# A hybrid decoder block on one core: projections as one plain float32 product in pairs of 64 columns, in place of three fp32r passes

## The reference

```python
h = rms_norm(x, mix_norm_w[l])
proj = h @ w_in[l]                      # 1024 x 7744: z, xbc, dt, q, k/v pairs, gates
y_ssm = mamba2_mixer(z, xbc, dt_raw, ...)
y_nsa = nsa_mixer(q, k_c, v_c, k_s, v_s, k_w, v_w, nsa_gate, ...)
g_ssm, g_nsa = jnp.split(jax.nn.sigmoid(merge_gate), 2, axis=-1)
merged = g_ssm * (y_ssm @ w_branch_ssm[l]) + g_nsa * (y_nsa @ w_branch_nsa[l])
x = x + merged @ w_out[l]
h = rms_norm(x, ffn_norm_w[l])
x = x + moe_ffn(h, ...)                 # 32 experts: top 4 of each token, gate_up 1024x2048, down 1024x1024
```

## Time and profile before

| | us |
|---|---|
| median of 3 runs | 1250.74 |
| lowest, highest | 1250.71, 1251.38 |
| profiled execution, its own time | 1250.38 |
| its span, first to last instruction | 1248.7 |

### The profile page before, as it was taken

One profiled execution on the slowest core, in us unless ns is written; L12 is line 12 of the kernel. 1 busy time (PEld: TensorE's weight loads), 2 busy tenths in 40 slices (PEclk: granted clock), 3 DMA queues, 4 the chain that ended last, 5 costly groups with the idle time before them and its releaser, 6 DMA issues.

```text
span 1248.7 us, 16280 instructions
## 1 busy us (share of the span) xinstructions
PE 1189.7 (95%) x6644; PEld 623.0 (50%) x6644; DVE 437.2 (35%) x869; ACT 287.7 (23%) x521; POOL 110.4 (9%) x97
## 2 busy tenths in 40 slices
PE   8999999999999999999898989899999999999996
PEld 8999988788743434433342424333343434243432
DVE  7776667767331231312122221212221212122212
ACT  6574457653410101101010100010110101010112
POOL 2302213345400000000000000000000000000000
PEclk9999999999999999999999999999999999999999
DMA  8747434339999999999999999999999999999996
GB/s 272 209 145 233 161 110 135 102 103 393 398 421 400 435 415 433 432 429 430 434 430 434 430 434 429 431 434 431 434 428 434 431 431 432 430 436 428 424 428 248
DMA packets 61565, 453.58 MB, mean 363 GB/s; under 512 B 9160, under 2 KB 33872, under 8 KB 45392
## 3 DMA queue, kind: packets, MB, share of 16 engines
q1 hardware_dynamic: 61216, 452.75, 88.3%
q10 hardware_dynamic: 304, 0.20, 0.1%
HBM read 451.88 MB, written 1.05 MB: 363 GB/s over the span
## 4 chain that ended last, share of the span: by engine, by line
PE 63%; DMA 29%; DVE 3%; ACT 3%; issue 1%; POOL 0%; SPq 0%; DVEq 0%; ACTq 0%
PE psum L1311 23%; DMA ring<-in_w_gate_up_dram 14%; DMA slot<-in_w_gate_up_dram 12%; PE psum L1323 11%; PE psum L940 9%; PE psum L1281 5%; PE psum L906 4%; PE psum L1349 3%; PE psum L842 3%; DMA ring<-in_w_down_dram 3%; PE psum L943 2%; ACT WH L1482 1%; ACT XDT L1661 1%; PE psum L1191 1%; DVE XDT L2139 1%
## 5 line engine op out<-in xcount | busy, mean ns | idle before, releaser
L1311 PE MATMUL psum<-ring,ZS 128*64 128x512 f32 x1512 | 344.7, 600 | 13.9 <-DMA ring<-in_w_gate_up_dram 13.5
L1311 PEld LDWEIGHTS psum<-ring,ZS 128*64 128x64 f32 x1512 | 105.0, 137 | 217.2 <-issue 194.3
L2285 DVE TENSOR_TENSOR X<-X,psum 128x1024 f32<-128x1024 f32 x62 | 72.9, 1217 | 370.8 <-PE psum L1349 370.7
L1323 PE MATMUL psum<-ring,HT 128*64 128x512 f32 x736 | 173.3, 625 | 22.6 <-DMA ring<-in_w_down_dram 22.6
L2267 DVE TENSOR_SCALAR ZS<-psum 128x512 f32<-128x512 f32 x32 | 22.1, 691 | 300.9 <-PE psum L1311 300.9
L1311 PE MATMUL psum<-slot,ZS 128*64 128x512 f32 x512 | 116.5, 597 | 7.7 <-DMA slot<-in_w_gate_up_dram 7.7
L1323 PEld LDWEIGHTS psum<-ring,HT 128*64 128x64 f32 x736 | 59.1, 143 | 129.5 <-issue 128.6
L1799 DVE TENSOR_TENSOR WL<-ring,WH 128x2048 fp32r<-128x2048 f32 (+1 forms) x42 | 95.9, 2285 | 37.9 <-ACT WH L1482 37.6
L1711 ACT ACTIVATE HT<-psum 128x512 f32<-128x512 f32 x31 | 18.5, 597 | 318.2 <-PE psum L842 318.2
L1482 ACT ACTIVATE WH<-ring 128x2048 fp32r<-128x2048 f32 (+1 forms) x42 | 78.9, 1878 | 9.8 <-PE psum L906 6.8
L1311 PEld LDWEIGHTS psum<-slot,ZS 128*64 128x64 f32 x512 | 34.4, 137 | 74.2 <-issue 58.8
(11 more groups left out here) (380 smaller groups left out, 1215.8 us busy)
## 6 DMA issues: line engine op xcount, KB each, us to landing
ring<-in_w_gate_up_dram SPq DMA_DIRECT2D x38, 4096.0 KB, 29.4
ring<-in_w_down_dram SPq DMA_DIRECT2D x18, 4096.0 KB, 30.8
slot<-in_w_gate_up_dram SPq DMA_DIRECT2D x12, 4096.0 KB, 28.9
ring<-in_w_gate_up_dram SPq DMA_DIRECT2D x15, 2048.0 KB, 13.4
ring<-in_w_in_dram SPq DMA_DIRECT2D x29, 1024.0 KB, 7.2
slot<-in_w_down_dram SPq DMA_DIRECT2D x7, 4096.0 KB, 30.8
ring<-in_w_down_dram SPq DMA_DIRECT2D x9, 2048.0 KB, 14.7
slot<-in_w_gate_up_dram SPq DMA_DIRECT2D x8, 2048.0 KB, 13.8
```

Source lines behind the costliest of these rows:

```text
L1311: ins = mm(psum[64 * (c % 2):64 * (c % 2) + 64, c // 2, :], XTS[:, k, s], every_other_run(row, c), start=False, stop=(k == KT - 1))
L1323: ins = mm(psum[64 * h:64 * h + 64, 2, :], lhs, w[:, at:at + 512], start=(k == 0), stop=(k == 7))
L2285: v.tensor_tensor(xo, xo, psum[:, 3 + 2 * t:5 + 2 * t, :], ALU.add).then_inc(o_read, 1)
```

## The change

All three-pass projections become one plain float32 product, with the stationary operand cut in two halves of 64 columns that write partitions 0 to 63 and 64 to 127 of the same bank. The splits on ScalarE and VectorE go, with their buffers, tokens and semaphores. The other float32 matmuls with 128 stationary columns named above are cut the same way. SyncE waits for a unit to be done before it loads its slot again, and issues four expert loads of 2 MB among the projection loads, at `mg` 4, `mg` 6, `bs` 0 and `bs` 2; the other early expert loads go out later in the order.

```diff
                 if u >= STREAM:
-                    if u - STREAM in SPLIT_UNITS:
-                        low_ready(sp, SPLIT_UNITS.index(u - STREAM))
-                    else:
-                        sp.wait_ge(unit_done, u - STREAM + 1)
+                    sp.wait_ge(unit_done, u - STREAM + 1)
                 full = ring_full[u % STREAM]
+                if (kind, m) in ahead:
+                    ahead[(kind, m)]()
...
+            ahead = {("mg", 4): lambda: load_half(gate_up_rows(0, 1), 1, 0),
+                     ("mg", 6): lambda: load_half(gate_up_rows(0, 1), 1, 1),
+                     ("bs", 0): lambda: early_load(1, 0), ("bs", 2): lambda: early_load(1, 1)}
...
             sp.wait_ge(pool_set, 3)
             sp.dma_start(once_row, unit_rows(3, 0, 4)[:, 2048:2 * 2048]).then_inc(once_full, 16)
-            sp.wait_ge(unit_done, at_unit[("bn", 3)] + 1)
-            load_half(gate_up_rows(0, 1), 1, 0)
-            low_ready(sp, len(SPLIT_UNITS) - 3)
-            low_ready(sp, len(SPLIT_UNITS) - 2)
-            early_load(0, 1)
             sp.wait_ge(mt_full, 4)
             once_quarter(0)
-            sp.wait_ge(unit_done, at_unit[("wo", 1)] + 1)
-            early_load(1, 0)
-            low_ready(sp, len(SPLIT_UNITS) - 4)
-            low_ready(sp, len(SPLIT_UNITS) - 1)
+            sp.wait_ge(unit_done, at_unit[("wo", 2)] + 1)
+            early_load(0, 1)
+            sp.wait_ge(unit_done, NU)
             early_load(0, 0)
-            sp.wait_ge(unit_done, at_unit[("wo", 2)] + 1)
-            early_load(1, 1)
-            sp.wait_ge(unit_done, NU)
-            load_half(gate_up_rows(0, 1), 1, 1)
...
                 if t == 0:
-                    pe.wait_ge(wh_ready, i + 2)
-                for n, (w, src) in enumerate([(wh, high), (wh, low), (wl, high)]):
-                    if w is wl and t == 0:
-                        low_ready(pe, i)
-                    if n == 1 and kind == "wo":
-                        pe.wait_ge(mt_low, 2 * h + t + 1)
-                    for k in range(4):
-                        ins = mm(bank(b, 512), src[:, 4 * h + k, P * t:P * t + P], w[:, k, :],
-                                 start=(h == 0 and n == 0 and k == 0), stop=(h == 1 and n == 2 and k == 3))
+                    pe.wait_ge(ring_full[u % STREAM], full_at[u])
+                for k in range(4):
+                    for c in (0, 64):
+                        ins = mm(bank(b, 512)[c:c + 64], src[:, 4 * h + k, P * t + c:P * t + c + 64], w[:, k, :],
+                                 start=(h == 0 and k == 0), stop=(h == 1 and k == 3))
...
+                thirds = (0, 3, 6, KT)
+                for k in range(thirds[n0], thirds[n1]):
+                    for c in (0, 64):
+                        at = slice(P * half + c, P * half + c + 64)
                         if feature_major:
-                            ins = mm(bank(b, 2, SEQ)[:, half], w[:, k, rows], src[:, k, :],
-                                     start=(n == 0 and k == 0), stop=(n == 2 and k == KT - 1))
+                            ins = mm(bank(b, 2, SEQ)[c:c + 64, half], w[:, k, at], HTH[:, k, :],
+                                     start=(k == 0), stop=(k == KT - 1))
...
-                mm(bank(7, SEQ), HTH[:, 0, 0:P], HTH[:, 1, :], start=True, stop=True)
+                mm(bank(7, SEQ)[0:64], HTH[:, 0, 0:64], HTH[:, 1, :], start=True, stop=True)
...
-            def split(u):
-
-                i = SPLIT_UNITS.index(u)
-                act.wait_ge(ring_full[u % STREAM], full_at[u])
-                if i >= SPLITS:
-                    act.wait_ge(unit_done, SPLIT_UNITS[i - SPLITS] + 1)
-                n = KT * (64 if UNITS[u][0] == "small" else 256)
-                a(WH[i % SPLITS][:, 0:n], slot_view(u, n), ACT.Copy).then_inc(wh_ready, 1)
...
-            def split(u):
-
-                i = SPLIT_UNITS.index(u)
-                dve.wait_ge(wh_ready, i + 2)
-                n = KT * (64 if UNITS[u][0] == "small" else 256)
-                v.tensor_tensor(WL[i % SPLITS][:, 0:n], slot_view(u, n), WHF[i % SPLITS][:, 0:n], ALU.subtract
-                                ).then_inc(wl_ready, 1)
...
```

More of the change, by code:

```diff
@@ L78 @@
 NU = len(UNITS)
-SPLIT_UNITS = [u for u, (kind, _) in enumerate(UNITS) if kind not in ("w1k", "w1v")]
 def wide(u):
@@ L165, in token_order @@
     out += [("H0", last), ("XX", 2), ("H1", last), ("RM", 2), ("P0", last), ("X3", 0), ("P1", last)]
[L168 to L178, removed]
-        else:
[L180 to L187, removed]
+    return out
 TOKENS = token_order()
@@ L286, in hybrid_block @@
         slot_at = [ring_at + 4 * SLOT * i for i in range(RING)]
[L287 to L298, removed]
+        HTH = at_place("HTH", [P, KT, SEQ], ht_at, F32)
+        OTH = at_place("OTH", [P, KT, SEQ], zs_at, F32)
+        YSH = at_place("YSH", [P, KT, SEQ], ec_at, F32)
         places = [at_place("slot0", [P, BIG], xdt_at + 4 * D, F32)[:]]
@@ L857, in first_unit @@
             def first_unit():
-                b = bank_of[0]
-                wh, wl = part(WH[0], 0, KT, 256), part(WL[0], 0, KT, 256)
+                b, w = bank_of[0], slot_view(0, KT, 256)
                 for part_n in range(2):
[L862 to L878, removed]
+                    pe.wait_ge((first_in, ring_full[0])[part_n], 16)
+                    for k in range(4 * part_n, 4 * part_n + 4):
+                        pe.wait_ge(ht_act, k // 2 + 1)
+                        for half in range(2):
+                            for c in (0, 64):
+                                ins = mm(bank(b, 2, SEQ)[c:c + 64, half], w[:, k, P * half + c:P * half + c + 64],
+                                         HTH[:, k, :], start=(k == 0 and half == 0), stop=(k == KT - 1),
+                                         skip_group_check=True)
+                    if part_n == 0:
+                        pe.wait_ge(mix_ready, 1)
+                        pe.wait_ge(rows_in, 16 * 5)
+                        tr(bank(4, P), PR[:]).then_inc(par_full, 1)
                 ins.then_inc(unit_done, 1)
@@ L924, in half_unit @@
                 feature_major = kind in ("xbc", "kc", "vc", "ks", "kw", "q", "z")
-                high, low = (HTH, MTL) if kind == "wo" else (HTH, HTL)
-                rows = slice(P * half, P * half + P)
                 nco = 256
-                i = SPLIT_UNITS.index(u)
-                wh, wl = part(WH[i % SPLITS], 0, KT, nco), part(WL[i % SPLITS], 0, KT, nco)
+                w = slot_view(u, KT, nco)
                 if half == 0 and n0 == 0:
-                    pe.wait_ge(wh_ready, i + 2)
-                passes = [(wh, high), (wh, low), (wl, high)]
-                for n in range(n0, n1):
-                    w, src = passes[n]
-                    if w is wl and half == 0:
-                        low_ready(pe, i)
-                    for k in range(KT):
+                    pe.wait_ge(ring_full[u % STREAM], full_at[u])
+                thirds = (0, 3, 6, KT)
+                for k in range(thirds[n0], thirds[n1]):
+                    for c in (0, 64):
+                        at = slice(P * half + c, P * half + c + 64)
                         if feature_major:
-                            ins = mm(bank(b, 2, SEQ)[:, half], w[:, k, rows], src[:, k, :],
-                                     start=(n == 0 and k == 0), stop=(n == 2 and k == KT - 1))
-                        else:
-                            ins = mm(bank(b, 2, nco)[:, half], src[:, k, rows], w[:, k, :],
-                                     start=(n == 0 and k == 0), stop=(n == 2 and k == KT - 1))
+                            ins = mm(bank(b, 2, SEQ)[c:c + 64, half], w[:, k, at], HTH[:, k, :],
+                                     start=(k == 0), stop=(k == KT - 1))
+                        else:
+                            ins = mm(bank(b, 2, nco)[c:c + 64, half], HTH[:, k, at], w[:, k, :],
+                                     start=(k == 0), stop=(k == KT - 1))
                 if half == 1 and n1 == 3:
@@ L957, in small_unit @@
             def small_unit(u):
-                b, i = bank_of[u], SPLIT_UNITS.index(u)
+                b = bank_of[u]
                 pe.wait_ge(proj_free[b], freed[u])
-                wh, wl = part(WH[i % SPLITS], 0, KT, 64), part(WL[i % SPLITS], 0, KT, 64)
-                pe.wait_ge(wh_ready, i + 2)
-                for n, (w, src) in enumerate([(wh, HTH), (wh, HTL), (wl, HTH)]):
-                    if w is wl:
-                        low_ready(pe, i)
-                    for k in range(KT):
-                        ins = mm(psum[0:64, b, 0:SEQ], w[:, k, :], src[:, k, :],
-                                 start=(n == 0 and k == 0), stop=(n == 2 and k == KT - 1))
+                w = slot_view(u, KT, 64)
+                pe.wait_ge(ring_full[u % STREAM], full_at[u])
+                for k in range(KT):
+                    ins = mm(psum[0:64, b, 0:SEQ], w[:, k, :], HTH[:, k, :], start=(k == 0), stop=(k == KT - 1))
                 ins.then_inc(unit_done, 1)
```

(22 more changed lines are left out.)

114 lines of the change are left out of this document (35 added, 79 removed).

## The result

The changed kernel takes 1307.13 us (median of 4 runs, 1306.86 to 1308.31) beside 1250.72 for the kernel before on the same chip: 1.0453 times as long, 95% interval 1.0434 to 1.0471. The forecast was 1317, the range 1300 to 1332.

The account below looks back on a forecast made before the run. TensorE was taken to bound the front, and the experts' start to fix the end; 31.4 + 0.9 + 28.1 + 0.8 + 0.9 - 2 + 0 + 5.6 + 1 = 66.7 us on 1250.38 gave 1317 us, range 1300 to 1332.

Parts of the forecast that it names:

- the vector engines' relief: VectorE and ScalarE in the front: removing 92.9 us of subtractions and 78.2 of copies saves only 2 us, at most 4.
- The 256-column halves: Projection half units of 256 columns: 2.875 us becomes 32 instructions in 3.56 us, 46 times, +31.4 us.
- The wide halves: Projection half units of 512 moving columns: 2.73 us becomes 16 instructions in 3.51 us, 36 times, +28.1 us.
- Part 4: Array form changes on TensorE before the experts: 47 more at 0.12 us each, +5.6 us.
- The changes of shape and the waits: TensorE in the front: 47 more array form changes, +5.6 us; idle time caused by the splits goes, -2 us.
- First unit, small unit, fill: First projection unit +0.9 us, small unit with lone instructions +0.8, four matmuls filling a wait before the last router step +0.9.
- The other float32 matmuls: Gathers, scores, states, C times B and sums of squares, only cut in two: 0 us, with 2 us to either side.
- Loads: Ring loads cost 0; early expert loads and DMA gaps at the experts' start together +1 us net, from -4 to +5.
- the faster pair: Rival for the projections: a pair costs half the price charged, so about 1170 us; chance 0.05.
- the shared operand: Rival for the projections: pairs sharing their moving operand overlap incompletely; 1347 us with a tenth added, about 1610 without overlap; chance 0.08.
- The vector chain as the true bound: Rival for 163 to 242 us: the vector chain, not TensorE, bounds there, giving 1286 us; chance 0.05.

Follow-up runs that it names:

- the cut alone: Kernel before with only gathers, scores, state blocks, C times B and sums of squares cut in pairs, projections unchanged: 1252.79 us beside 1250.57.
- two passes: Kernel before with the high-by-low pass left out of every unit but the first and the small one, splits kept: 1235.05 us, 0.9876.

## Why the prediction was right, and where its sizes were off

The mechanism held at each step: TensorE sets the front, plain float32 asks more of it than three fp32r passes, the vector engines' relief is hidden, and the end follows the start of the experts by a fixed distance (912 us predicted, 912.0 measured). The sum was 66.7 us, the spans differ by 56.7. The ten microseconds lie in these terms:

- *The 256-column halves, +31.4 predicted, +26.1 measured.* This is the largest miss. I drew a straight line between 57.0 ns at 128 columns and 219.4 at 512 and took 111.2; it is 108.0. Both ends of the line were too high, because both rows stand behind another array form and include the entry. In the changed kernel the compressed-block run of L965 comes behind projections of its own form and takes 3.49 us, 54.5 ns an instruction, instead of 3.65. The price at 512 is 214.6. The line between 54.5 and 214.6 gives 107.9.
- *The wide halves, +28.1 predicted.* The price of 219.4 ns held the same 0.15 us of entry, which Part 4 then charged once more. A half costs 3.43 us and not 3.51, so 36 of them grow by 25.3 us. The trace of the kernel before had shown it already: the run of L1323 below comes behind L1311, of its own form, and L1311 of the earlier trace rows behind another.

```profile
396.76 6.87 PE psum L1323 x32
```

- *The changes of shape and the waits, 5.6 - 2 predicted.* The transposes got 4.4 us longer, and the head broadcasts with C times B 1.4. But the wide halves paid for changes before as well: 102.7 us for 36 at 2.73 is 4.4 on top, 126.9 for 36 at a third of 10.30 is 3.3, which makes +24.2 in all. The value products and scores got 1.9 shorter. TensorE's own waits between the start-up and the last one before the experts fell from 1.9 us in all to 0.4, near the 2 us taken off. Adding the new changes to prices that held old ones counted them twice. The wide halves and these groups together give 28.1 us, where I had 31.7; the groups that the table leaves out took some 0.3 back.
- *First unit, small unit, fill: +0.9, +0.8, +0.9 predicted, +1.0, +0.7, +1.0 measured.* The small unit shows that a lone instruction costs twice the paired one, as I inferred: 3.45 us for 16, 216 ns. The pairs' common moving operand did them no harm.
- *The other float32 matmuls, 0 predicted.* Scores -0.7 us, the gather in pairs 3.49 us (3.77 before) in the hidden stage. In the cut alone, where its changes of shape come among whole projections, +2.2 us.
- *Loads, +1 predicted, 0.2 measured.* The ring loads were never waited for. DMA did idle at the start of the experts, 381 GB/s in 27.6 us, as the sum said, but it cost next to nothing.

Of the rivals, the faster pair fell with whole matmuls at the same price, and the shared operand with 108.0 ns. The vector chain as the true bound fell in its strong form: TensorE has no gap there. But two passes show that the next bound lay only some 19 us below and was not confined to the stretch from 163 to 242 us. Had the change made TensorE faster instead of slower, the prediction would have missed by much for that.

What stays open: how the 0.09 to 0.19 us spread over the kinds of changes comes from a few rows only, and which of the waits on ScalarE, VectorE and the clock absorbed most of the 58 us with two passes was not tried.

## What to carry to other kernels

Before replacing several cheap passes by one dear one, count array time, not matmuls: three fp32r passes cost 360 ns for a 128-column step of 256, one plain float32 product 432, cut in pairs or not. Pairs of column halves pay where the matmul was only 64 wide to begin with, and then only if neighbours alternate between the halves. Read a price from a run that stands behind work of its own form; a row that includes the entry from another form must not be added to a separate term for changes. Find the event that fixes the rest of the program (here the start of the experts), and price a change by what it does to that event; the freed vector time and the earlier loads brought about 2 us and nothing measurable here.

## What the runs showed of the hardware beyond what I expected

- Matmuls of the same column half in a row cost 216 ns each at 256 float32 columns (3.45 us for 16), alternating ones 108. At the border between two runs of different halves nearly four of them overlap, so that a half unit taken apart costs 6.1 us and not 6.9.
- A whole float32 matmul costs what its pair costs, at 256 moving columns (6.91 us for a unit either way) and at 512 (6.87 us for two whole halves, 10.30 for three paired ones).
- The same work costs more behind another form of the array: 0.15 us for paired projections (7.06 beside 6.91, 7.02 beside 6.87), 0.09 to 0.19 us in the rows of the cuts alone.
